# Six modulation buffers instead of four, their loads placed differently in SyncE's queue, and two reorderings around the norms, in a two-layer SGU / pooling / PEER kernel

## What is computed

```python
mod = silu(c) @ ada_w[i] + ada_b[i]              # six chunks of 1024 per layer
h   = rmsnorm(x) * norm1_g * (1 + mod[1]) + mod[0]
# layer 0: spatial gating
z = gelu(h @ w_in); u, v = z[:, :2048], z[:, 2048:]
v = rmsnorm(v, v_gain); sv = w_s @ v + b_s
x = x + mod[2] * ((u * sv) @ w_out)
# layer 1: pooling: x + mod[2] * (group(pool(h @ w_in)) @ w_out)
f = rmsnorm(x) * norm2_g * (1 + mod[4]) + mod[3]
x = x + mod[5] * peer(f)                          # 16384 experts, top 16 of 8 heads
out = rmsnorm(x) * final_gain
```

## Time and profile before

| | |
|---|---|
| median of three runs | 1863.58 us |
| lowest, highest | 1859.71, 1865.44 us |
| the profiled execution | 1865.96 us |
| its span in the profile | 1864.2 us |
| TensorE busy | 1840.4 us (99%) |
| VectorE busy | 1508.8 us (81%) |
| ScalarE busy | 962.6 us (52%) |
| GpSimd busy | 447.7 us (24%) |
| DMA | 376.33 MB, mean 202 GB/s |

### The profile page before, as it was taken

One profiled execution on the slowest core, in us unless ns is written; L12 is line 12 of the kernel. 1 busy time (PEld: TensorE's weight loads), 2 busy tenths in 40 slices (PEclk: granted clock), 3 DMA queues, 4 the chain that ended last, 5 costly groups with the idle time before them and its releaser, 6 DMA issues.

```text
span 1864.2 us, 35462 instructions
## 1 busy us (share of the span) xinstructions
PE 1840.4 (99%) x11760; PEld 1585.6 (85%) x11760; DVE 1508.8 (81%) x2800; ACT 962.6 (52%) x1608; POOL 447.7 (24%) x225
## 2 busy tenths in 40 slices
PE   8999999999999999999999999999999999999998
PEld 7899998888888888888888998888888888878887
DVE  7684789978998888888888588997999888886555
ACT  6554455655555444445555445565555544445554
POOL 6136578870000000000001258884000000000000
PEclk9999999999999999999999999999999999999999
DMA  8866455556645555588874445556555555555554
GB/s 340 315 240 225 159 179 183 189 187 210 214 169 174 176 170 179 169 293 319 319 285 159 147 160 190 182 189 204 203 203 172 173 174 174 175 169 192 191 192 134
DMA packets 104177, 376.33 MB, mean 202 GB/s; under 512 B 12464, under 2 KB 12464, under 8 KB 103856
## 3 DMA queue, kind: packets, MB, share of 16 engines
q1 hardware_dynamic: 103392, 373.37, 58.7%
q0 software_dynamic: 432, 2.10, 0.3%
q10 hardware_dynamic: 288, 0.06, 0.0%
HBM read 374.43 MB, written 1.05 MB: 201 GB/s over the span
## 4 chain that ended last, share of the span: by engine, by line
PE 90%; DVE 4%; DMA 3%; ACT 1%; POOL 1%; issue 1%; SPq 0%; ACTq 0%; DVEq 0%; POOLq 0%
PE ring L1778 22%; PE O L1833 13%; PE O L1835 12%; PE O L1834 12%; PE ring L1780 11%; PE ring L1750 3%; PE ring L1493 2%; PE ring L1495 2%; PE ring L1494 2%; PE ring L1771 2%; DMA raw<-in_u 1%; PE O L1771 1%; PE ring L1752 1%; DVE wL L901 1%; ACT wH L532 1%; PE O L1623 1%
## 5 line engine op out<-in xcount | busy, mean ns | idle before, releaser
L532 ACT ACTIVATE wH<-raw 128x1024 fp32r<-128x1024 f32 x597 | 634.3, 1062 | 818.1 <-DMA raw<-in_v 366.0
L1778 PE MATMUL ring<-hX,wH 128*128 128x512 f32 x1984 | 704.3, 399 | 0.1
L901 DVE TENSOR_TENSOR wL<-raw,wH 128x1024 fp32r<-128x1024 f32 x384 | 470.3, 1225 | 174.2 <-ACT wH L532 170.4
L1780 PE MATMUL ring<-hX,wL 128*128 128x256 f32 x1984 | 555.1, 280 | 0.0
L1778 PEld LDWEIGHTS ring<-hX,wH 128*128 128x128 f32 x1984 | 372.5, 188 | 86.9 <-issue 0.9
L1833 PE MATMUL O<-wH,gateH 128*128 128x512 f32 x1024 | 405.1, 396 | 0.0
L1835 PE MATMUL O<-wH,gateL 128*128 128x512 f32 x1024 | 399.5, 390 | 0.0
L1834 PE MATMUL O<-wL,gateH 128*128 128x512 f32 x1024 | 398.3, 389 | 0.0
L1780 PEld LDWEIGHTS ring<-hX,wL 128*128 128x128 f32 x1984 | 374.6, 189 | 0.0
L494 POOL TENSOR_TENSOR wL<-raw,wH 128x1024 fp32r<-128x1024 f32 x128 | 316.8, 2477 | 54.8 <-ACT wH L532 53.7
L1835 PEld LDWEIGHTS O<-wH,gateL 128*128 128x128 f32 x1024 | 192.2, 188 | 41.4
(11 more groups left out here) (213 smaller groups left out, 2419.6 us busy)
## 6 DMA issues: line engine op xcount, KB each, us to landing
raw<-in_u SPq DMA_DIRECT2D x256, 512.0 KB, 3.3
raw<-in_v SPq DMA_DIRECT2D x256, 512.0 KB, 3.3
ada_v<-in_ada SPq DMA_DIRECT2D x40, 512.0 KB, 4.4
raw<-in_w_q SPq DMA_DIRECT2D x30, 512.0 KB, 3.3
ada_m<-in_ada SPq DMA_DIRECT2D x24, 512.0 KB, 5.2
raw<-in_w_in SPq DMA_DIRECT2D x23, 512.0 KB, 4.5
ada_f<-in_ada SPq DMA_DIRECT2D x16, 512.0 KB, 15.1
raw<-in_w_out SPq DMA_DIRECT2D x16, 512.0 KB, 4.0
```

Source lines behind the costliest of these rows:

```text
L532: nc.scalar.activation(wH[s % RAW][:, :], (place or raw[s % RAW])[:, :], ACT.Copy).then_inc(s_h, 1)
L901: nc.vector.tensor_tensor(wL[s % RAW][:, :], raw[s % RAW][:, :], wH[s % RAW][:, :].bitcast(fp32), ALU.subtract).then_inc(s_low, 1)
L1778: mm(bank[:, :], wH[s][:, k * P:k * P + P], hX[:, k, :, :].rearrange("p two t -> p (two t)"), start=(k == 0), stop=False)
L1780: ins = mm(bank[:, 0:T], wL[s][:, k * P:k * P + P], hH[:, k, :], start=False, stop=(k == KT - 1))
```

## The change

1. In the front loop (L1014), in step k = 2, `low_h(0, 1)` comes first on VectorE, and the six remaining `rooted(j)` products follow it instead of going ahead of it.
2. The ring `ada_m` has six buffers. To make room, one of the nine `front_raw` buffers (w_v tile 11) is now `ada_f[0]`, and two others have moved. Tiles 16 to 19 and the small constants are loaded right behind the front's loads, ahead of w_v tile 12; tiles 20 and 21 behind w_v tile 15; twelve more beside W_U tiles 0, 2 to 6 and 8 to 13; six beside W_OUT tiles 3, 5, 7, 9, 11 and 12. A load of m from 20 on waits for VectorE to be done with m - 6. VectorE uses its W_U share in steps 0 to 2 and 4 to 8 instead of 0 to 7.
3. The load of `keys` goes from between W_U and W_OUT to behind the first four `w_q` tiles, with a wait for the ring, whose place it takes. TensorE waits for it at the first score instead of in the norm.
4. At `norm(2)` ScalarE makes the eight squares before the high part of p_in tile 2, and VectorE makes its low part inside the norm, behind `scaled(5)`, instead of ahead of the reciprocal.

```diff
-        for under, count in ((64, 4), (88, 2), (100, 3)):
+        for under, count in ((64, 4), (88, 2), (104, 2)):
...
+        front_raw.append(ada_f[0])
...
-            ada_m = [sb(f"ada_m{x}", [P, D], at=ad) for x in range(4)]
+            ada_m = [sb(f"ada_m{x}", [P, D], at=ad) for x in range(6)]
...
+        U_LOADS = (0, 2, 3, 4, 5, 6, 8, 9, 10, 11, 12, 13)
+        U_ADA = (0, 1, 2, 4, 5, 6, 7, 8)
+        OUT_LOADS = (3, 5, 7, 9, 11, 12)
...
+            def load_early(m):
+
+                if m >= ADA_FRONT + 4:
+                    sp.wait_ge(s_acc, m - 6 + 1)
+                sp.dma_start(ada_m[gate_slot(m)][:, :], ada_d[m]).then_inc(s_gates[gate_slot(m)], 16)
...
-            m = ADA_FRONT
+            for m in range(ADA_FRONT, ADA_FRONT + 4):
+                load_early(m)
+            for dst, src in small_loads:
+                sp.dma_start(dst, src).then_inc(s_small, 16)
             for t in range(BLOCK_TILES, 16):
                 load_gate(t)
-                load_ada(ada_m, m, first=True)
+            m = ADA_FRONT + 4
+            for t in range(2):
+                load_early(m)
                 m += 1
-            load(stream_dram["w_u", 0], W_U, 0, 0)
-            for dst, src in small_loads:
-                sp.dma_start(dst, src).then_inc(s_small, 16)
             for t in range(16):
-                if t:
-                    load(stream_dram["w_u", 0], W_U, t // 4, t % 4)
-                if t < 8 or t > 11:
-                    load_ada(ada_m, m)
+                load(stream_dram["w_u", 0], W_U, t // 4, t % 4)
+                if t in U_LOADS:
+                    load_early(m)
                     m += 1
-            sp.dma_start(keys[:, 0], k1_d[0]).then_inc(s_keys, 16)
-            sp.dma_start(keys[:, 1], k2_d[0]).then_inc(s_keys, 16)
             for t in range(16):
                 load(stream_dram["w_out", 0], W_OUT, t // 4, t % 4)
-                if 4 < t < 13:
-                    load_ada(ada_m, m)
+                if t in OUT_LOADS:
+                    load_early(m)
                     m += 1
...
                     if layer == 0:
+                        sp.wait_ge(s_acc, ADA_U0)
+                        sp.dma_start(keys[:, 0], k1_d[0]).then_inc(s_keys, 16)
+                        sp.dma_start(keys[:, 1], k2_d[0]).then_inc(s_keys, 16)
...
-                if layer < LAYERS - 1:
-                    ahead(base, 31, 3)
                 for j in range(KT):
                     act.wait_ge(s_res, KT * layer + j + 1)
                     square(j)
+                if layer < LAYERS - 1:
+                    ahead(base, 31, 3)
                 norm(2 * layer + 2)
...
                     if k == 3 and n % 2:
                         low_first(BASE["w_q", n // 2], 0, 2)
+                    if k == 3 and n == 2:
+                        low_first(BASE["p_in", 1], 0, 2)
...
-                elif k == 2:
+                else:
+                    low_h(0, k - 1)
+                if k == 2:
                     for j in range(2, KT):
                         last = rooted(j)
                     nc.vector.memset(tick[:, 0:1], 0.0).then_inc(s_rooted, 1)
-                    low_h(0, 1)
-                else:
-                    low_h(0, k - 1)
...
-                        if t < 8:
-                            ada_tile(ada_m, m)
+                        if t in U_ADA:
+                            ada_early(m)
...
-                if layer == 0:
-                    low_first(base, 31, 6)
                 norm(2 * layer + 2)
```

More of the change, by code:

```diff
@@ L158, in build @@
                 front_raw += [sb(f"front_raw{under}_{x}", [P, D], at=fr) for x in range(count)]
+        front_raw.append(ada_f[0])
         with ExitStack() as ad:
-            sb("under_ada_m", [P, 112 * T], at=ad)
-            ada_m = [sb(f"ada_m{x}", [P, D], at=ad) for x in range(4)]
+            sb("under_ada_m", [P, 104 * T], at=ad)
+            ada_m = [sb(f"ada_m{x}", [P, D], at=ad) for x in range(6)]
         with ExitStack() as ad:
@@ L199, in build @@
         s_ada = [sem(f"s_ada{x}") for x in range(4)]
+        s_gates = [sem(f"s_gates{x}") for x in range(6)]
         s_front = [sem(f"s_front{x}") for x in range(16)]
@@ L299, in build, with gate_slot @@
         ADA_U = (ADA_U0, ADA_U1)
+        U_LOADS = (0, 2, 3, 4, 5, 6, 8, 9, 10, 11, 12, 13)
+        U_ADA = (0, 1, 2, 4, 5, 6, 7, 8)
+        OUT_LOADS = (3, 5, 7, 9, 11, 12)
+        def gate_slot(m):
+            return (m - ADA_FRONT + 2) % 6
         ADA_END = 12 * KT
@@ L348, in load, with load_ada @@
                 sp.dma_start(raw[s % RAW][:, :], tile).then_inc(s_raw[s % RAW], 16)
-            def load_ada(place, m, first=False):
-                if not first:
-                    sp.wait_ge(s_acc, m - len(place) + 1)
+            def load_early(m):
+                if m >= ADA_FRONT + 4:
+                    sp.wait_ge(s_acc, m - 6 + 1)
+                sp.dma_start(ada_m[gate_slot(m)][:, :], ada_d[m]).then_inc(s_gates[gate_slot(m)], 16)
+            def load_ada(place, m):
+                sp.wait_ge(s_acc, m - len(place) + 1)
                 sp.dma_start(place[m % len(place)][:, :], ada_d[m]).then_inc(s_ada[m % 4], 16)
@@ L362, in load_gate @@
                 if t in FRONT_RAW:
+                    if t == FRONT_RAW[-1]:
+                        sp.wait_ge(s_acc, 1)
                     sp.dma_start(front_raw[t - 3][:, :], stream_dram["w_v", 0][t]).then_inc(s_fraw[t - 3], 16)
@@ L924, in ada_front, with ada_tile, ada_early @@
                 add_ada_psum(ada_f[n], n // 2 + (KT, 0)[n % 2])
-            def ada_tile(place, m, psum=False):
-                dve.wait_ge(s_ada[m % 4], 16 * ((m - ADA_FRONT) // 4 + 1))
-                (add_ada_psum if psum else add_ada)(place[m % len(place)], m)
+            def ada_tile(place, m):
+                dve.wait_ge(s_ada[m % 4], 16 * ((m - ADA_U0) // 4 + 1))
+                add_ada(place[m % len(place)], m)
+            def ada_early(m, psum=False):
+                dve.wait_ge(s_gates[gate_slot(m)], 16 * ((m - ADA_FRONT + 2) // 6 + (gate_slot(m) > 1)))
+                (add_ada_psum if psum else add_ada)(ada_m[gate_slot(m)], m)
             def modulations(lo_chunk, hi_chunk, norms, unit=None):
@@ L1102, in _ @@
                             for _ in range(OUT_ADA[2 * j + s]):
-                                ada_tile(ada_m, m, psum=True)
+                                ada_early(m, psum=True)
                                 m += 1
@@ L1613, in scores @@
             def scores(layer, j):
+                if layer == 0 and j == 0:
+                    pe.wait_ge(s_keys, 32)
                 if j < QUERY_NARROW:
@@ L1722, in _ @@
                         mean(3, j - 2)
-                if layer == 0:
-                    pe.wait_ge(s_keys, 32)
                 n = 2 * layer + 1
```

## The result

The changed kernel takes 1867.89 us (median of 20 runs, 1864.65 to 1871.83) against 1863.83 us of the kernel before on the same chips (20 runs, 1859.71 to 1868.12). The ratio is 1.0022, with a 95% interval of 1.0014 to 1.0029: slower by some 4 us, where 1853.9, ten less, was forecast. The profiled span is 1867.0 us against 1864.2.

What follows compares the result with a forecast made beforehand. TensorE was busy 1840.4 of 1864.2 us, so only its 23.8 us idle and slow stretches could be had. 1.8 + 5.4 - 0.3 + 2.8 + 0.0 = 9.7 us off the median 1863.58 gave 1853.9, range 1849.7 to 1859.8.

Steps and rivals of the forecast that it cites:

- SyncE's new waits: In W_U, waits for VectorE's products hold back weight loads, tightest at tile 27, but hidden; 0.3 us deducted with the norm of v.
- part 2b: W_U tile 1: its load lands earlier, so the 3.7 us wait and the slow stretch of 1.7 go, 5.4 us gained.
- Term: +2.8 forecast: W_OUT: tile 0 comes 2.3 us earlier and the 1.3 and 1.7 us waits go; 2.8 us gained, bounds 1.0 to 3.0.
- F: Rival, chance 0.05: DMA binds in W_U, every tile is late, waits and slow stretches cost 17 us, giving 1870.9.
- B: Rival, chance 0.15: front gives nothing, clock halves at 26 to 28, tile 12 late, norm(2) costs 0.6; 1856.3.
- the price of a `low_h` under GpSimd: At norm(2): a `low_h` meeting GpSimd takes 1.34 us instead of 0.47; two such cost 0.9 to 1.2 each.
- part 2a: Loads ahead of w_v tile 12: it lands between 50.3 and 51.3, leaving 1.8 of the front's 2.7 us.
- The clock stayed up: Front, before w_v tile 3: the clock stays up after 1.6 us of idle, as behind the 1.7 us wait.
- The norm of v: In W_U, next in line to be late, but fits with 0.7 to 1.0 us to spare.

Runs made afterwards that it cites:

- e1: Changed kernel with the six W_OUT modulation loads beside tiles 6, 7, 8, 9, 11, 12; 1860.18 us, 0.9987 of the kernel before.
- e7: Changed kernel with W_OUT loads beside tiles 6, 7, 8, 9, 11, 12 and only ScalarE's norm(2) order as before; 1854.24 us, 0.9956 of the kernel before.
- e6: Kernel before with part 4 of the change alone; 1866.89 us, 1.0015 of the kernel before.
- e9: Kernel of e7 with part 1 of the change undone; 1857.88 us, 0.9968 of the kernel before.
- e4: Changed kernel with only the first W_OUT modulation load one step later, beside tile 4; 1864.86 us, 1.0010 of the kernel before.
- e10: Kernel of e7 with the four tiny arrays issued from GpSimd's queue at its start; 1858.38 us, 0.9964 of the kernel before.
- e2: Changed kernel with part 4 undone; 1865.03 us, 1.0016 of the kernel before.
- e3: Kernel of e1 with part 4 undone; 1857.27 us, 0.9970 of the kernel before.
- e5: Kernel before with part 1 of the change alone; 1863.58 us, 0.9995 of the kernel before.

## Why the prediction was wrong

- **The failed step is the one on SyncE's new waits in part 2b.** It said that they "hold back the weight loads queued behind", which was right, named tile 27 in W_U as the tightest, and looked at W_U alone. The tightest is tile 34 in W_OUT. Tile by tile the rule was at hand: m waits for product m - 6, the eight products of W_U end with 27, so tile 34 waits for the first product of W_OUT, and that stands in VectorE's program behind all of the low parts `gL`. In the kernel before, the first load of W_OUT stood beside tile 5. Term: +2.8 forecast, -4.9 measured; e1 gives the forecast's sign back (+3.4 against before), and the difference, 8.3, is what the held queue costs.
- **The rivals.** F alone had the right sign, and came nearest (1870.9), by the wrong mechanism: the DMA engines did not bind, they stood at 0 GB/s behind a waiting queue. B had two places right, a front that gives nothing with tile 12 landing late, and a norm(2) that turns against the kernel; its slow clock at 26 to 28 did not come, and its 0.6 for norm(2) was too little. None of the rivals had SyncE's queue as the bound.
- **Part 4** (0.0 forecast, bounds +1.3 and -0.6; -2.2 measured). The gain was real and rightly sized: e7 has it, 1.4. The failed step is the price of a `low_h` under GpSimd, 1.34 from the earlier trace rows. The row of the same place, showed 4.29 us for one low part under the same three GpSimd operations, and the prediction even wrote that they "held it". It took the row from the front, where GpSimd's operations stood two in a row, over the one of norm(2). A price near the 3.40 us that came was to be had from that row, and no bound reached it.
- **Part 1 and part 2a** (+1.8 forecast, -0.7 measured). Tile 3 came as forecast, 28.06 for 27.8. That TensorE then runs "2.7 us earlier than before" up to tile 12 was wrong in two steps: GpSimd's chain from tile 3 on, which ran without a gap before, now stood for ScalarE's high parts (1.79 and 0.48 us, behind 2.39 ahead of tile 3), TensorE had a wait of 0.87 for a `low_h` of 1.61 us beside GpSimd, and by tile 11 0.1 us was left (less than nothing in the other profiles with part 1); and tile 12 landed at 53.34, not 50.3 to 51.3, since the sum went by the mean stream and left out the 2.3 us from there to the landing. The clock stayed up, as taken.
- **Part 2b in W_U** was right: 5.4 forecast for the wait and its slow stretch, less 0.3; from W_U 0 to W_OUT 0 it gave 5.9, of which the forecast counted the last part under W_OUT. The norm of v had no wait in it.
- **The sum** comes near in e7, in which the two mistakes are mended (8.2 us by the ratio for 9.7), but not term by term, and the nearness is in part luck. By the stages of its profile against before, the front costs 1.2 us (forecast: it gives 1.8), W_U gives 6.2 (5.1), W_OUT 3.7 (2.8) and norm(2) 1.4 (0.0).

The Trainium skill ("SBUF — State Buffer", section "SBUF: two separate sides") has the port pair held for a whole instruction. In the front the trace of the kernel after agrees: the `low_h` of 1.61 us waited for about one GpSimd operation of 1.3 us. At norm(2) it does not agree as a price: between GpSimd's operations of the same 128 x 512 the waiting VectorE operation did not get its turn, and its price was the rest of the row (it took 3.40 and 4.29 us), not the rest of one instruction of 1.24 us. What sets the two places apart was not tried.

Open: what sets off the slower clock. The 2.6 us wait of the front was followed by 0.50 in before and e6, and not in e9; that of norm(2) was in after, e4 and e6, and not in e1. Open too is what set back the W_U loads in e10. And with one profile a kernel, 2.5 us of spread between the first score and norm(2) lies over every sum of spans; the stage lengths above are free of it.

## What to carry to other kernels

When a load with a wait is moved up in a queue, write down for each such load which instruction frees its place, where that stands in its own engine's program, and which loads queue behind the wait: one entry that is one stage too early (8.7 us of a standing queue) outweighed all the gains of the others. Price a collision by the row of the same place and the same partners, even if it looks like an exception: the same `low_h` cost 1.61 us beside GpSimd in the front and 3.40 at norm(2). When transfers are summed up, end at the landing, not at the last byte.

## What the runs showed of the hardware

- A VectorE operation can wait for a whole row of GpSimd operations on 128 x 512. At norm(2) it did in every profile in which they met: 3.40 us (after, e1), 3.39 (e4, e6), 4.13 (e2), 4.11 (e3), 4.29 (before), 4.28 (e5) for operations of 0.47 and 0.68, with GpSimd's three taking 3.7. With GpSimd's row over first, 0.49 and 0.68 (e7). In the front, inside rows of six such operations, it waited for one: 1.60 to 1.62 us for a `low_h` in all ten profiles in which they met.
- In a full DMA queue a load of 512 KB landed some 2.3 us later than the bytes summed up to it; the packets of four tiny arrays of 4 to 8 KB took 0.35 us of the DMA engines' time together, and the landing behind them was the same with them in the queue (51.3 to 52.0) and with them sent earlier (51.7).
- TensorE's clock fell to 0.50 for 6.8 us at a wait of 5.9 (after) and also at one of 2.9 (e4), in both beginning inside the wait. Another wait of 2.9, in W_U of e6, and the 3.7 of before were followed by 3.4 us, and a wait of 2.6 by 3.4 us in some executions and by none in others.
- The root of the first norm starts at 11.59 to 12.83 us in six kernels whose front is the same program (after, e1 to e4, e7), each profiled once, and from there to W_U they take 54.0 to 54.8 us: up to 0.8 us of a front's length are no effect of an edit.
